# A four-layer mixer network on one core: the first layer's modulation, norm and key/value steps in another order

## The reference, cut to what matters

```
def modulation(cvec, w_ada, b_ada):
    return jnp.split(jax.nn.silu(cvec) @ w_ada + b_ada, 3, axis=-1)
...
for i in range(DEPTH):
    sh_l, sc_l, gt_l = modulation(c, w_ada, b_ada)
    sh_c, sc_c, gt_c = modulation(c_ctx, w_ada, b_ada)
    h_l = rmsnorm(x_lat, g_pre) * (1.0 + sc_l[:, None, :]) + sh_l[:, None, :]
    h_c = rmsnorm(x_ctx, g_pre) * (1.0 + sc_c) + sh_c
    y_l, y_c = mixer(h_l, h_c, need_ctx=need_ctx)
```

## Time and profile before

| what | value |
|---|---|
| median of 3 runs | 1538.76 us (1526.81 to 1539.01) |
| the profiled execution | 1540.94 us, of which the span of instructions is 1539.1 us |
| mean granted TensorE clock | 0.989 |
| PE busy | 1457.3 us, 95% |
| DVE busy | 995.4 us, 65% |
| ACT busy | 758.4 us, 49% |
| HBM read | 199.43 MB |

### The profile page before, as it was taken

The page is one execution under the profiler, slowest core; times in us unless marked ns, Lnnn a source line. Parts: engine busy times, 40 slices in busy tenths (PEclk is TensorE's granted clock), DMA queues, the critical chain, the costliest instruction groups (busy, mean ns, idle before and its releaser), DMA issues.

```text
span 1539.1 us, 24150 instructions
## 1 busy us (share of the span) xinstructions
PE 1457.3 (95%) x9368; PEld 1201.8 (78%) x9368; DVE 995.4 (65%) x2319; ACT 758.4 (49%) x1672; POOL 70.9 (5%) x82
## 2 busy tenths in 40 slices
PE   6999999999999999999989999998999899899999
PEld 4787767787778777888767777676787799799987
DVE  4647677664667548545585678767867567777753
ACT  4445566453655443241233546756666347555542
POOL 0000000110000100020000100001101020000000
PEclk9999999999999999999999999999999999999999
DMA  9132270322740322222451155334544632445554
GB/s 366 58 109 83 100 270 2 103 83 69 257 168 1 110 89 83 96 83 82 171 199 55 55 177 142 109 105 130 171 141 148 215 132 97 164 154 189 187 186 135
DMA packets 58882, 202.84 MB, mean 132 GB/s; under 512 B 6818, under 2 KB 9930, under 8 KB 58640
## 3 DMA queue, kind: packets, MB, share of 16 engines
q1 hardware_dynamic: 52928, 192.84, 36.3%
q10 hardware_dynamic: 5440, 7.07, 2.0%
q0 software_dynamic: 400, 1.38, 0.4%
HBM read 199.43 MB, written 1.84 MB: 131 GB/s over the span
## 4 chain that ended last, share of the span: by engine, by line
PE 70%; DVE 16%; ACT 5%; issue 3%; DMA 3%; POOL 2%; SPq 0%; ACTq 0%; DVEq 0%; POOLq 0%
PE ps L2281 65%; PE ps L2284 5%; DVE w_l L2944 4%; DVE st L3051 2%; ACT w_h L2598 1%; DMA w_l_ada<-in_l_ada 1%; DVE l_P L2948 1%; ACT l_P L2601 1%; DVE x L2952 1%; DVE l_h_lat L2952 1%; DVE m_P L3535 1%; DMA w_raw<-in_l_out 1%; POOL mstat L3629 1%; DVE l_xn L2948 1%; POOL pstat L3640 1%
## 5 line engine op out<-in xcount | busy, mean ns | idle before, releaser
L2944 DVE TENSOR_TENSOR w_l<-w_raw,w_h 128x1024 fp32r<-128x1024 f32 (+3 forms) x263 | 315.7, 1207 | 76.6 <-ACT w_h L2598 76.0
L2598 ACT ACTIVATE w_h<-w_raw 128x1024 fp32r<-128x1024 f32 (+3 forms) x263 | 272.3, 1042 | 99.4 <-DMA w_raw<-in_f_down 25.3
L2281 PE MATMUL ps<-w_h,l_hTh 128*128 128x512 f32 (+1 forms) x384 | 156.3, 407 | 1.3 <-DVE w_l L2944 0.6
L2281 PE MATMUL ps<-w_l,l_hTh 128*128 128x512 f32 (+1 forms) x384 | 151.7, 395 | 0.0
L2281 PE MATMUL ps<-w_h,l_hTl 128*128 128x512 f32 (+1 forms) x384 | 151.5, 395 | 0.0
L2601 ACT ACTIVATE l_P<-ps,st 128x512 f32<-128x512 f32 (+1 forms) x128 | 77.6, 608 | 87.7 <-DVE st L2952 60.1
L2281 PE MATMUL ps<-f_hTh,w_l 128*128 128x256 f32 x352 | 99.3, 282 | 0.0
L2281 PE MATMUL ps<-f_hTh,w_h 128*128 128x256 f32 x352 | 99.2, 282 | 0.0
L2281 PE MATMUL ps<-f_hTl,w_h 128*128 128x256 f32 x352 | 98.9, 281 | 0.0
L2281 PE MATMUL ps<-l_hTh,w_h 128*128 128x512 f32 (+1 forms) x264 | 97.0, 367 | 0.6 <-issue 0.6
L2281 PE MATMUL ps<-l_hTl,w_h 128*128 128x512 f32 (+1 forms) x264 | 96.5, 365 | 0.0
(11 more groups left out here) (449 smaller groups left out, 3456.4 us busy)
## 6 DMA issues: line engine op xcount, KB each, us to landing
w_two<-in_l_ada SPq DMA_DIRECT2D x24, 1024.0 KB, 6.8
w_raw<-in_l_z SPq DMA_DIRECT2D x32, 512.0 KB, 3.6
w_two<-in_l_adg SPq DMA_DIRECT2D x16, 1024.0 KB, 5.7
w_raw<-in_l_out SPq DMA_DIRECT2D x32, 512.0 KB, 3.7
w_raw<-in_m_merge SPq DMA_DIRECT2D x24, 512.0 KB, 3.4
w_raw<-in_f_gate SPq DMA_DIRECT2D x22, 512.0 KB, 3.4
w_raw<-in_f_up SPq DMA_DIRECT2D x22, 512.0 KB, 3.7
w_raw<-in_f_down SPq DMA_DIRECT2D x22, 512.0 KB, 4.3
```

Source lines behind the costliest of these rows:

```text
L2281: return p.e.matmul(out, lhsT, rhs, start=start, stop=stop)
L2598: return p.e.activation(out, a, func, scale=scale)
L2944: return p.e.tensor_tensor(out, a, b, op)
```

## The change

It reorders steps in `layer_first`, and nothing else. The group g0 is turned and added, and the latent rows of kp 0 are transposed and modulated, ahead of the norm of context tile 3. In the loop the conditioning blocks no longer come in fours ahead of a group: steps of one or two blocks lie between single tiles of the key/value product, of which the first two tiles come one round earlier than before.

```
         p.ahead = 0
-        for t in LAT + CTX:
+        for t in LAT + CTX[:1]:
             drain(upto(mod, 1))
             r.norm((t,))
+        drain(upto(mod, 1))
+        late.pop()()
+        r.at(LAT, 0)
         p.W.split_more()
+        r.norm(CTX[1:])
         p.cond_mask()
         p.i_tok.append(("begin", "mask"))
         m.start()
-        for kp in range(4):
-            if kp:
-                drain(upto(mod, 4))
-                p.W.split_more()
+        drain(upto(mod, 2))
+        r.at(CTX, 0)
+        drain(upto(mod, 1))
+        drain(upto(kv, 2))
+        for kp in range(1, 4):
+            drain(upto(mod, 1))
+            p.W.split_more()
+            drain(upto(kv, 1))
             late.pop()()
             r.at(LAT, kp)
+            drain(upto(kv, 1))
+            drain(upto(mod, 2 if kp < 3 else 0))
             r.at(CTX, kp)
-            if kp:
-                drain(upto(kv, 4))
+            drain(upto(mod, 1 if kp < 3 else 0))
+            drain(upto(kv, 2))
         p.W.split_more()
         drain(kv)
         p.W.split_more(2)
```

## The result

The changed kernel is slower by a little: the median of 22 runs is 1540.99 us (1536.4 to 1548.97), that of the kernel before, run beside it, 1536.57 (1526.81 to 1542.9, 22 runs). The ratio is 1.0029 with a 95% interval of 1.0016 to 1.0041, so 2.5 to 6.3 us. The kernel before was measured again beside every batch of experiments and had medians of 1538.18 to 1538.89 there, up to 2.3 us above this one; a ratio is therefore always to the runs taken beside it. The profiled execution took 1542.03 us, with a span of 1540.2 and a mean granted clock of 0.991.

The account below looks back on a forecast made before the run. PE bounds the kernel (95% busy), with the load of b7 holding the start until 22.59 us. Adding 0.45 us at kv3 and 1.27 at the keys gives 1.7 us slower, about 1540 us, range 1525 to 1547.

Parts of the forecast that it names:

- the late context tile: Front: PE turns context tile 3 at 22.45 us, not 18.93; first key/value matmul at 23.9.
- the slow array: Front: PE at 1.2 GHz until about 26.4 us, six of twelve matmuls slow, ending at 27.85 instead of 26.7.
- the key chain: Inside kv3: a DVE subtraction ahead of the second tile's key rotation delays the keys by 1.27 us.
- The wait of g3: Before kv3: ACT and DVE late with kp 3's rows, kv3 at 49.4 us in effect, 0.45 later than today.
- the sum up to kv3: From 27.85 us: blocks 3.8, matmuls 14.0, turns and transposes 2.9, giving 48.55 against 48.93 today.
- the inner range: Whole time 1536.5 to 1545.5 us, from the ends of the clock, kv3 wait and key chain terms.
- Nothing beyond 60 us: Rest of the span: time after 60 us is a plain shift of the one before.
- the first (the front's gain survives): Rival: array fast by 24 us, kp 3 in time, kv3 at 47.3; 1537.5 us, chance 0.2.
- The second: Rival: later stretches of low granted clock decide, landing as in the 1526.81 run; 1528 us, chance 0.15.
- The third: Rival: array at 1.2 GHz through b7 and rest of kv0, 2.1 us more; 1542.6 us, chance 0.12.
- The fourth: Rival: no effect, front DMA-bound until b7 in any order, PE work the same; 1538.8 us, chance 0.08.

Follow-up runs that it names:

- experiment 7: Changed kernel with the ring's rounding and subtraction moved from inside kv3 to behind it; ratio 1.0015 to the kernel before.
- experiment 3: Changed kernel with the ring's rounding and subtraction moved from inside kv3 to ahead of its first tile; ratio 1.0034 to the kernel before.
- Experiment 5: Changed kernel plus 34 unused identity transposes in PE's waits for loads before the first key/value matmul; ratio 1.001 to the kernel before.
- Experiment 4: Kernel before with blocks b8 to b15 each behind one key/value tile instead of in fours; ratio 1.0015 to the kernel before.
- experiment 1: Changed kernel's order up to b6, with the loop of the kernel before behind it; ratio 1.0006 to the kernel before.
- experiment 9: Kernel before's front, two early key/value tiles, reordered loop with blocks in fours, plus 23 unused identity transposes in load waits; ratio 1.0008 to the kernel before.

## Why the prediction was right or wrong

The forecast was 1.7 us slower, the result 4.5 by the runs and 4.60 by the key turn. The direction held, and so did three mechanisms: the late context tile, the slow array and the key chain. The wait of g3 didn't come, and single blocks cost what was not in the sum. Of the 2.9 us by which the forecast was short, the clock makes 1.0, the sum up to kv3 2.6 and the key chain 0.1, less 0.85 for g3.

That 1540 stands so near the measured 1540.99 is luck in part. The forecast was built on the median of three runs, 1538.76; the 22 runs beside the changed kernel had 1536.57, so the start was 2.2 us too high and the step 2.9 us too small. The 1% that I took for what a measurement can tell was too wide as well: the interval of the ratio is 0.25% wide. And the inner range, 1536.5 to 1545.5, isn't one sum: from 1540.5 its upper end adds the key chain's 2.3 in full, though 1.27 of it is already in the forecast.

- **Context tile 3 is later**: forecast at 22.45, it came at 22.86, or 22.32 without the 0.54 us by which b3 was late. Right.
- **The clock**: I counted six of the first twelve matmuls at the lower level; the spacing shows nine (24.70 to 28.28), and b6 took 1.01 us until the first matmul and not 0.63, the upper pace, though my own count had the array low there. The end of the twelve came 1.0 us later than forecast (28.85 without the jitter, against 27.85). Right in kind, mis-sized by that. Two things were wrong in it. I had today's array low until 23.3 where b7 shows it low until 23.7. And a fixed stretch of steady work is no measure: with the same instructions on PE six, nine and ten of the twelve were slow in three traces (experiment 7, the changed kernel, experiment 3), so that six would have been right for one of them. The rule of the Trainium skill ("TensorE: Matmul & The Clock Gate", section "Loop structure matters more than you think") on loops that wait for a DMA between bursts held in this kernel. Experiment 5 shows it as cause, with 2.33 us at kv3.
- **The sum up to kv3** is where the largest error lies. From the end of the twelve I had 20.7 us to kv3 and it took 23.3. The term "nine blocks at 0.42 each" took the pace of blocks among their like for blocks standing alone; a block alone takes 0.57, a pair 1.01, and the matmul behind it 0.1 more. Experiment 4 measures 0.20 to 0.25 us per single block. So the three saved waits of 0.40 are paid for again: a round is 0.2 us longer than before, not 0.4 shorter.
- **g3 late by ACT and DVE**: forecast 0.85 us between 48.55 and 49.4. It didn't happen beyond 0.1 (kv3's third matmul stands 0.33 behind the second and not 0.23, and DVE's low part for it ends at 53.26, just before its start at 53.32). PE itself was three microseconds later by then, and DVE's three subtractions took the time that I counted (3.49 us against 3.7) but were over 0.23 us before the turn's result was there for `ada_add`:

```profile
46.74 3.49 DVE L2954 TENSOR_TENSOR w_l<-w_raw,w_h 128x1024 fp32r<-128x1024 f32 x3
50.46 0.23 DVE L2954 TENSOR_TENSOR mod<-ps,col 128x4 f32<-128x4 f32 x2 [0.23 <-PE ps L2294]
```

- **The key chain**: forecast 1.27, measured 1.39 (8.77 against 7.38 from kv3), and experiment 7, with DVE's rows, shows the subtraction as cause of 1.13 of it. Right.
- **Nothing beyond 60 us**: not shown. From the key turn to the end the profiled executions have 1482.8 us before and 1478.7 after, so the later part is 4 us shorter in the changed one and no plain shift. Their mean granted clocks, 0.989 and 0.991, are worth about 17 and 14 us of lost clock, which is 3 of the 4. What speaks for a mere shift is that the shift at the key turn (4.60) and that of the runs (2.5 to 6.3) agree.
- **The rivals**: the first (the front's gain survives) fails by experiment 1, which puts 2.69 us of loss on the front alone. The second did not decide. The third was in its near half right: more matmuls at 1.2 GHz than counted. The fourth, that nothing changes, fails by both measures: the interval of the ratio lies above 1, and the key turn is 4.60 us later.

## What to carry to other kernels

Before work is moved into an engine's waits, ask what the engine does between: on PE a row of short bursts between landings kept the array at its lower clock level here, and what was saved in waiting was lost in pace. Price a moved instruction by the row in which it stands in its new company, not by the one where it stood among its like. And when PE nowhere waits for the split of its operands, find out which work covers that path before taking the work away.

## What the runs showed of the hardware that I had not expected

- **The clock column at the start.** In the changed kernel the column prints 1.00 from 20 to 25 us, though transposes and matmuls run at half pace there; in experiment 9, where the array had already come up and fell again, the same column prints the lower level.

```profile
20.00:25.00 5.00, 4.05 (x45) 2.17 (x38) 3.10 (x8) 2.55 (x7) 0.55 (x1) 1.00 1.04 411
```

```profile
20.00:24.00 4.00, 2.05 (x51) 1.19 (x49) 2.76 (x9) 1.90 (x4) 0.00 (x0) 1.00 1.02 405
24.00:28.00 4.00, 4.00 (x16) 3.09 (x12) 1.33 (x3) 0.03 (x1) 0.00 (x0) 0.59 1.03 410
```

  So ahead of the first change of level the column can't be trusted, and the spacing of equal instructions can (0.43 or 0.23 us for 512 columns).

- **A conditioning block taken alone costs 0.20 to 0.25 us more than one among its like** (experiment 4), where matmuls with 32-column weights and with 128-column weights alternate: the first 512-column matmul behind either kind of neighbour takes 0.31 to 0.34 us to the next one, and the last instruction ahead of a block 0.33.
- **The same start does not always come up to speed at the same place.** The changed kernel and those of experiments 3 and 7 have the same instructions on PE until kv3; nine of the first key/value matmuls were at the lower level in the first, ten and six in the others, and kv3 lies at 37.19, 37.41 and 36.65. Single traces tell the clock term only to some 0.8 us.
